# Four gated input products: one 512-column moving operand for the high weight block, the two result halves added when PSUM is emptied

## The reference, cut to what matters

```python
def swiglu_2(x, w_gate, w_up, w_down):
    return (jax.nn.silu(x @ w_gate) * (x @ w_up)) @ w_down

    x = x + 0.5 * swiglu_2(rmsnorm_2(x, ffn1_norm), ffn1_gate, ffn1_up, ffn1_down)
    ...
    x = x + 0.5 * swiglu_2(rmsnorm_2(x, ffn2_norm), ffn2_gate, ffn2_up, ffn2_down)
```

## Time and profile before

| | |
|---|---|
| Time, median of 3 runs | 2870.36 us (2867.75 to 2871.41) |
| Span of the profiled execution | 2866.6 us; the median is 3.8 us above it, for what lies around the span and for the spread of runs |
| TensorE matmuls | busy 2796.4 us (98%), 23696 |
| TensorE weight loads | busy 2684.6 us (94%), 23696 |
| VectorE, ScalarE, GpSimd | 64%, 47%, 28% |

### The profile page before, as it was taken

One profiled execution on the slowest core, in us unless ns is written; L12 is line 12 of the kernel. 1 busy time (PEld: TensorE's weight loads), 2 busy tenths in 40 slices (PEclk: granted clock), 3 DMA queues, 4 the chain that ended last, 5 costly groups with the idle time before them and its releaser, 6 DMA issues.

```text
span 2866.6 us, 59491 instructions
## 1 busy us (share of the span) xinstructions
PE 2796.4 (98%) x23696; PEld 2684.6 (94%) x23696; DVE 1820.9 (64%) x2505; ACT 1341.1 (47%) x1872; POOL 789.2 (28%) x768
## 2 busy tenths in 40 slices
PE   6999999999999999999999999999999999999999
PEld 4999999999999999999987898999889999997999
DVE  4655746687647557566466765665876566488664
ACT  3434434444435444344345444445764444377443
POOL 1322411123304214133001330320743223146330
PEclk9999999999999999999999999999999999999999
DMA  8765666575666756766631454555325555541554
GB/s 304 256 243 205 231 232 209 193 248 193 235 233 204 243 202 209 240 201 230 239 104 60 147 183 154 176 193 184 131 82 186 195 174 184 192 156 60 178 183 152
DMA packets 151712, 546.44 MB, mean 191 GB/s; under 512 B 16688, under 2 KB 20576, under 8 KB 151136
## 3 DMA queue, kind: packets, MB, share of 16 engines
q1 hardware_dynamic: 147632, 534.84, 54.9%
q10 hardware_dynamic: 3888, 8.86, 0.9%
HBM read 541.80 MB, written 1.84 MB: 190 GB/s over the span
## 4 chain that ended last, share of the span: by engine, by line
PE 91%; DVE 5%; ACT 1%; issue 1%; ACTq 1%; DMA 0%; SPq 0%; DVEq 0%
PE ps L410 28%; PE ps L412 28%; PE ps L411 28%; PE ps L437 2%; DVE w_lo L390 1%; PE ps L821 1%; PE ps L805 1%; PE ps L794 1%; ACTq L1558 0%; DVE xT L1952 0%; DVE h_lo L1602 0%; DVE xT L1968 0%; PE ps L889 0%; PE ps L696 0%; DVE m L1967 0%
## 5 line engine op out<-in xcount | busy, mean ns | idle before, releaser
L390 DVE TENSOR_TENSOR w_lo<-raw,w_hi 128x1024 fp32r<-128x1024 f32 x874 | 1135.4, 1315 | 634.5 <-ACT w_hi L382 632.1
L410 PE MATMUL ps<-h_hi,w_hi 128*128 128x256 f32 (+1 forms) x4928 | 1405.8, 285 | 24.3 <-DVE h_lo L1602 12.2
L412 PE MATMUL ps<-h_hi,w_lo 128*128 128x256 f32 (+1 forms) x4928 | 1393.8, 283 | 0.0
L411 PE MATMUL ps<-h_lo,w_hi 128*128 128x256 f32 (+1 forms) x4928 | 1388.5, 282 | 0.0
L382 ACT ACTIVATE w_hi<-raw 128x1024 fp32r<-128x1024 f32 x874 | 894.4, 1053 | 515.5 <-PE ps L412 514.5
L410 PEld LDWEIGHTS ps<-h_hi,w_hi 128*128 128x128 f32 x4928 | 929.9, 189 | 45.2 <-issue 25.2
L412 PEld LDWEIGHTS ps<-h_hi,w_lo 128*128 128x128 f32 x4928 | 947.9, 192 | 0.0
L411 PEld LDWEIGHTS ps<-h_lo,w_hi 128*128 128x128 f32 x4928 | 932.2, 189 | 0.8
L2266 POOL CAST u_hi<-ut 128x256 fp32r<-128x256 f32 (+1 forms) x258 | 234.3, 908 | 1370.4 <-DVE ut L1760 787.1
L410 PE MATMUL ps<-u_hi,w_hi 128*128 128x256 f32 (+1 forms) x2064 | 588.4, 285 | 0.2 <-DVE ut L1654 0.2
L411 PE MATMUL ps<-u_lo,w_hi 128*128 128x256 f32 (+1 forms) x2064 | 581.2, 282 | 0.0
(11 more groups left out here) (317 smaller groups left out, 1761.7 us busy)
## 6 DMA issues: line engine op xcount, KB each, us to landing
raw<-wst SPq DMA_DIRECT2D x874, 512.0 KB, 3.4
modraw<-wmod SPq DMA_DIRECT2D x132, 512.0 KB, 5.3
headraw<-wmod SPq DMA_DIRECT2D x12, 512.0 KB, 10.0
mtab<-mixtabs ACTq DMA_DIRECT2D x2, 1673.5 KB, 7.1
xT<-xin ACTq DMA_DIRECT2D x2, 1024.0 KB, 23.6
atab<-attabs ACTq DMA_DIRECT2D x1, 1024.0 KB, 6.2
out<-xT SPq DMA_DIRECT2D x1, 1024.0 KB, 4.8
skew<-sqb ACTq DMA_DIRECT2D x1, 768.0 KB, 3.3
```

Source lines behind the costliest of these rows:

```text
L390: dve.tensor_tensor(w_lo[:, s, :], raw[:, s, :], w_hi[:, s, :], ALU.subtract).then_inc(S("lo_ready"), 1)
L410: pe.matmul(psum, wh, hi, start=start, stop=False)
L411: pe.matmul(psum, wh, lo, start=False, stop=False)
L412: return pe.matmul(psum, wl, hi, start=False, stop=stop)
```

## The change

- The high and the low part of the state stand side by side in one buffer `h_parts[:, 2, DC, 2T]`; `h_hi` and `h_lo` are its halves.
- In the four gated stages without the "shift" columns (the four of the last two layers), `wide_tile` replaces `tile`: one matmul with the high weight block as stationary operand and both state parts as a moving operand of 2 x 256 columns, into a whole bank of 512 columns, and one matmul of 256 columns with the low weight block and the high state part, added to the bank's first half. The product is then the sum of the bank's two halves.
- When both units of a pair are done, ACT copies the two banks' second halves to SBUF (one instruction, 2x256 columns), DVE adds them to the first halves (one instruction), DVE multiplies both by `rstd` (one instruction), and then Silu and the gated product follow as before. `gt`, `ut` and `sq` become three parts of one buffer `gus`, so that gate and up can be reached by one instruction.
- The splits of the next weight units move: in these stages, ACT and DVE split units n+3 and n+4 when n units are done, so that the out stage's own splits begin three units later (`ahead=5`).
- The other four products of that kind of the first layers, the shifted stage and all out stages keep `tile`.

```diff
+        def wide_tile(pe, s, k, bank, both, start, stop):
+            wh, wl = w_hi[:, s, P * k:P * (k + 1)], w_lo[:, s, P * k:P * (k + 1)]
+            pe.matmul(ps[:, bank, :].rearrange("p (a t) -> p a t", a=2), wh, both, start=start, stop=False)
+            return pe.matmul(ps[:, bank, 0:T], wl, both[:, 0, :], start=False, stop=stop)
...
             def gu_pe(c, before):
                 N, b = c["N"] + 2 * c["shift"], c["unit"]
                 first_units(c, before[1])
+                if not c["shift"]:
+                    wide_unit(b + 2, 0, 2)
+                    wide_unit(b + 3, 0, 3)
+                    with pe.Fori(1, FC // 2) as i:
+                        for j in range(2):
+                            pe.wait_ge(S("sum_made"), FC * c["wide"] + 2 * i + (j - 1))
+                            wide_unit(b + 2 * j, i, 2 * j)
+                            wide_unit(b + 2 * j + 1, i, 2 * j + 1)
+                    return
...
+            def wide_gu_act(c):
+                b = c["unit"]
+                def pair(i, j, bank):
+                    act.wait_ge(S("unit_done"), b + 2 * j + 2 + 4 * i)
...
+                    act.activation(gus[:, 0:3:2, j, T:2 * T], ps[:, bank:bank + 2, T:2 * T],
+                                   ACT.Copy).then_inc(S("low_copied"), 1)
+                    split_hi(act, b + 2 * j + 5, i)
+                    act.wait_ge(S("gate_scaled"), FC * c["fin"] + 2 * i + (j + 1))
+                    act.activation(gt[:, j, 0:T], gt[:, j, 0:T], ACT.Silu).then_inc(S("silu_done"), 1)
+                    split_hi(act, b + 2 * j + 6, i)
...
+            def wide_gu_dve(c):
+                d, hid = c["unit"], c["hid"]
+                def pair(i, j, bank):
+                    both = gus[:, 0:3:2, j, 0:T]
+                    dve.wait_ge(S("low_copied"), FC * c["wide"] + 2 * i + (j + 1))
+                    dve.tensor_tensor(both, ps[:, bank:bank + 2, 0:T], gus[:, 0:3:2, j, T:2 * T],
+                                      ALU.add).then_inc(S("sum_made"), 1)
+                    dve.wait_ge(S("sum_made"), FC * c["wide"] + 2 * i + (j + 1))
+                    dve.tensor_tensor(both, both, rstd[:, 0:T].unsqueeze(1).broadcast_to([P, 2, T]),
+                                      ALU.mult).then_inc(S("gate_scaled"), 1)
+                    split_lo(dve, d + 2 * j + 5, i)
+                    dve.wait_ge(S("gate_scaled"), FC * c["fin"] + 2 * i + (j + 1))
+                    dve.wait_ge(S("silu_done"), FC * c["ffn"] + 2 * i + (j + 1))
+                    dve.wait_ge(S("ulo_ready"), hid + 2 * i + (j + 1))
+                    dve.tensor_tensor(ut[:, j, 0:T], gt[:, j, 0:T], sq[:, j, 0:T], ALU.mult).then_inc(S("gated"), 1)
+                    split_lo(dve, d + 2 * j + 6, i)
```

More of the change, by code:

```diff
@@ L140, in make_plan @@
     plan = []
-    c = dict(unit=REACHED["dense"], norm=0, pre2=0, x=0, out=0, post=0, ffn=REACHED["ffn"], fin=0,
+    c = dict(unit=REACHED["dense"], norm=0, pre2=0, x=0, out=0, post=0, ffn=REACHED["ffn"], fin=0, wide=0,
              hid=REACHED["hid"], h=0, early_n=0)
@@ L158, in gu, with out @@
         c["fin"] += 1
+        c["wide"] += not shift
         c["hid"] += FC
-    def out(N, nk):
-        add("out", N=N, nk=nk)
+    def out(N, nk, ahead=2):
+        add("out", N=N, nk=nk, ahead=ahead)
         c["unit"] += nk
@@ L186, in make_plan @@
                 gu(T)
-                out(T, FC)
+                out(T, FC, 5)
             else:
@@ L714, in first_units @@
                     for n in range(2):
[L715 removed]
+                        if c["shift"]:
+                            mm = tile(pe, (b + n) % RING, k, ps[:, 4 + n, 0:N], h_hi[:, k, 0:N], h_lo[:, k, 0:N], k == 0, k == DC - 1)
+                        else:
+                            mm = wide_tile(pe, (b + n) % RING, k, 4 + n, h_parts[:, :, k, 0:T], k == 0, k == DC - 1)
                         if k == DC - 1:
@@ L718, in first_units, with wide_unit @@
                 early_stat(norm)
+            def wide_unit(d, i, bank):
+                s = d % RING
+                pe.wait_ge(S("lo_ready"), d + 4 * i + 1)
+                for k in range(DC):
+                    mm = wide_tile(pe, s, k, bank, h_parts[:, :, k, 0:T], k == 0, k == DC - 1)
+                mm.then_inc(S("unit_done"), 1)
             def gu_pe(c, before):
@@ L1314, in first_qkv_act @@
                 hi_upto(act, d + 14)
+            def wide_gu_act(c):
+                b = c["unit"]
+                def pair(i, j, bank):
+                    act.wait_ge(S("unit_done"), b + 2 * j + 2 + 4 * i)
+                    if not isinstance(i, int):
+                        act.wait_ge(S("sum_made"), FC * c["wide"] + 2 * i + (j - 1))
+                    act.activation(gus[:, 0:3:2, j, T:2 * T], ps[:, bank:bank + 2, T:2 * T],
[4 more added lines that the diff above has]
+                    split_hi(act, b + 2 * j + 6, i)
+                pair(0, 0, 4)
+                pair(0, 1, 2)
+                with act.Fori(1, FC // 2) as i:
+                    for j in range(2):
+                        pair(i, j, 2 * j)
             def gu_act(c):
+                if not c["shift"]:
+                    wide_gu_act(c)
+                    return
                 b = c["unit"]
@@ L1336, in out_act @@
             def out_act(c):
-                b, nk = c["unit"], c["nk"]
-                full = nk // 4 if b + nk + 2 <= UNITS else (nk - 2) // 4
-                with act.Fori(0, full) as i:
+                b, first = c["unit"], c["unit"] + c["ahead"]
+                n = min(b + c["nk"] + 2, UNITS) - first
+                with act.Fori(0, n // 4) as i:
                     for j in range(4):
-                        split_hi(act, b + 2 + j, i)
-                for k in range(4 * full, nk):
-                    split_hi(act, b + 2 + k)
+                        split_hi(act, first + j, i)
+                for k in range(n // 4 * 4, n):
+                    split_hi(act, first + k)
             def post_act(c):
@@ L1618, in pre2_dve @@
                 recip(c, T)
+            def wide_gu_dve(c):
[14 more added lines that the diff above has]
+                    split_lo(dve, d + 2 * j + 6, i)
+                pair(0, 0, 4)
+                pair(0, 1, 2)
+                with dve.Fori(1, FC // 2) as i:
+                    for j in range(2):
+                        pair(i, j, 2 * j)
             def gu_dve(c):
+                if not c["shift"]:
+                    wide_gu_dve(c)
+                    return
                 d = c["unit"]
@@ L1807, in out_dve @@
             def out_dve(c):
-                b, nk = c["unit"], c["nk"]
-                full = nk // 4 if b + nk + 2 <= UNITS else (nk - 2) // 4
-                with dve.Fori(0, full) as i:
+                b, first = c["unit"], c["unit"] + c["ahead"]
+                n = min(b + c["nk"] + 2, UNITS) - first
+                with dve.Fori(0, n // 4) as i:
                     for j in range(4):
-                        split_lo(dve, b + 2 + j, i)
-                for k in range(4 * full, nk):
-                    split_lo(dve, b + 2 + k)
+                        split_lo(dve, first + j, i)
+                for k in range(n // 4 * 4, n):
+                    split_lo(dve, first + k)
             def post_dve(c, follower):
```

9 lines of the change are left out of this document (4 added, 5 removed).

## The result

The changed kernel takes 2875.64 us (median of 20 runs, 2868.89 to 2878.03), the kernel before 2870.03 (20 runs). The ratio is 1.0019, with a 95% interval of 1.0013 to 1.0025: slower by 5.6 us. The interval excludes 1, but 5.6 us is still just inside the 5.7 us (0.2%) that I had set as the least that can be told from no change. I had forecast 2858.1 us and 0.53 for faster.

The account below looks back on a forecast made before the run. TensorE was taken as the bound, its gated-stage matmuls paced by weight loads. Terms of -27.1, +11.4 and +3.4 us summed to -12.3, giving 2858.1 us; the forecast's own range was 2851 to 2866, with rivals 2847 to 2886.

Parts of the forecast that it names:

- Term 1: Gated stages: with loads hidden under the wide matmul, a block falls from 353.7 to 333.5 ns, -27.1 us in all.
- the loads set the 117.9 ns: Gated stages before: each 256-column matmul is bound by its weight load, 112 ns plus a hand-over of some 6 ns.
- The loads' 112 ns: Distance between weight-load starts at 64-column matmuls, taken as the least for 128x128 loads, above the 106.7 ns of 256 columns.
- half clock: At 1.2 GHz, 256-column fp32r matmuls start 0.21 to 0.22 us apart, read as the load's extra vanishing under longer columns.
- the extra belongs to each matmul: Gated stages: the wide matmul also keeps 11.2 ns extra; 11.3 ns saved a block, 2870 us, no change; chance 0.25.
- the moving reads set the pace: Gated stages: 512 columns take 235.8 ns, nothing saved, stage ends add 14.8 us, 2885 us; chance 0.15.
- The row with 258 columns: Profile row: 24 matmuls at 120.0 ns each, 2.1 ns more for two columns, noted as speaking against a load bound.
- Term 2: Within gated stages: DVE's 4.45 us and ACT's 3.11 us per pair fit in TensorE's 5.34 us; cost nothing.
- Term 3: Gated stage start: first pair's sum ends about 2148.0, before PE asks at 2148.7; cost nothing.
- Term 4: Gated stage ends: the longer chain to the gated product idles TensorE 2.85 us, four times, +11.4 us.
- Term 5: Behind the stage-end stalls: two of four bring 3.4 us of half clock, 1.7 us lost each, +3.4 us; bounds 0 to 6.8.
- the stall of 5.31 us: Earlier TensorE idle stretch, cited as being followed by 6.8 us at half clock when estimating the clock's loss.

Follow-up runs that it names:

- e10: Changed kernel with the wide matmul's weights cut to 32, 64, 96 and 128 columns in the four gated stages; stages took 116.6 to 118.0 us.
- e4: Changed kernel with the wide matmul reading a contiguous constant buffer of 264, 320, 384, 512 columns; 384 cost 290.3 ns a block, 512 cost 346.9.
- e2: Changed kernel with the wide matmul alone taken back, the two halves still added by ACT and DVE; 2881.85 us, ratio 1.0041.
- e1: Changed kernel with 24 out matmuls in place of 12 ahead of the wait for the gated product; 2863.18 us, ratio 0.9977 of the kernel before.
- e5: Changed kernel with VectorE's gated product moved ahead of the weight split in the wide gated stages; 2872.85 us in one execution.
- e6: Changed kernel with both 24 out matmuls ahead of the wait and the gated product ahead of the split; 2862.40 us, ratio 0.9975.
- e9: Changed kernel with the narrow matmul's weights cut to 32, 64, 96 and 128 columns in the four gated stages; stages took 116.6 to 118.0 us.

## Why the prediction was wrong, point by point

- **Term 1, wide matmuls: the step that failed.** I put -27.1 us; it is -8.95. The sum went wrong where it took the 215.6 ns of a full fp32 matmul for a fp32r one of 512 columns. It takes 230, so a block saves 6.7 ns and not 20.2. The reading behind it, that the loads set the 117.9 ns, was wrong too: e10 leaves 116 to 118 ns with a quarter of the load. The loads' 112 ns were a chance neighbour of 117.9. Nor did half clock speak for the loads, as I had read the earlier trace rows: in the kernel before, at a granted clock of 0.50, the loads between full fp32 matmuls of 64 columns start 0.21 us apart too (L1069 at 2639.72: four in 0.97 us, each 0.33 long), the distance of fp32r matmuls of 256 columns. And a column of full fp32 costs 0.84 ns in that kernel (L1041 at 2087.09 and 2089.68: 216 ns from start to start at 256 columns, 430 at 512), 1.9 times the 0.442 of fp32r in e4; that it passes twice for each load is what I read from 215.6 against 106.7 ns. The measured saving lies about midway between two rivals: 11.3 ns a block if the extra belongs to each matmul (wide 224 ns), nothing if the moving reads set the pace (wide 236 ns). A matmul of 512 columns costs some 6 ns less than two of 256. What the runs show is that most of the extra goes with the columns and not with the load or the pieces; that it is the reads which hold the columns up is not shown, for no run tells them from the writes into PSUM. The row with 258 columns had spoken against the loads, and I gave it too little weight, though its 120.0 ns are not on the line of e4 either (118.6).
- **Term 2, ACT and DVE within the stage:** right. e2 shows the stage unchanged to 0.01 us with all of the new work. e4 shows where it would end: below some 91 us a stage VectorE is the bound.
- **Term 3, the stage's start:** right. The trace has no wait of TensorE for the sum (`sum_made`).
- **Term 4, the stage's end:** the mechanism right and shown by e1 and e5. The added chain is 2.37 us, not 2.85: ACT starts 0.27 behind the first out matmul, not 0.38; the multiply starts 0.04 behind the add and not 0.21; and the rows of the weight split and of the product begin some 0.08 us before the row ahead of them ends. My aside that the chain would be 1.6 us shorter without the split in the way was wrong: e5 shows 0.4 to 0.5, since the product then waits for Silu (my own numbers, Silu to 3.06 us and the product behind it, gave 0.8).
- **Term 5, the clock:** I took two falls of four; there were three, each 3.4 us at half clock. With them the ends cost 14.0 us in this execution, against 14.8 forecast. That these are so near is luck in part: four chains 0.48 us too long make 1.9 us, and one fall too few makes 1.7 the other way. One reading was loose: of the 6.8 us at half clock behind the stall of 5.31 us TensorE worked only 5.15; the rest was idle.
- The time lies within my range, 2847 to 2886, but only because that rival's 2885 set its upper end; the direction, slower, is that of the rival, which I gave 0.15. By my own 5.7 us it counts as no difference, which I gave 0.26.

## What to carry to other kernels

A price for an operation that the trace lacks is best not taken from a neighbour that differs in type, even where its number fits a simple formula: one run with the operand's length varied would have told. When an evacuation grows by a few instructions, look at the one place where the next stage waits for the last of them: within the stages 0.7 us more per pair on VectorE and on ScalarE each were free, at their ends each tenth of a us was paid, and behind three of the four the granted clock was 0.50 for 3.4 us, an estimated 1.7 us each. Here the stall was cheap to cover (e1 and e6 are 12 to 13 us below the changed kernel by their ratios), by moving work of the next stage that doesn't need the late result ahead of the wait.

## What the runs showed of the hardware that I had not expected

- At a granted clock of 1.00 a fp32r matmul takes about 0.44 ns per column and some 5 ns (117 ns at 256, 230 at 512 columns), the wide one in one piece or in two, with 416 and 480 columns (187 and 219 ns) some ns above the line through their neighbours. It does not get shorter when the weight load beside it is cut from 128 to 32 columns (116 to 118 ns in e10, 230 to 235 in e9). At half clock nothing shows on top of the columns: wide and narrow take 0.43 and 0.21 us, 0.82 to 0.84 ns a column, in the changed kernel's first pair (the last row is the window of these and the next matmul, granted clock 0.50):

```profile
1789.69 0.63 PE L417 MATMUL ps<-h_parts,w_hi 128*128 128x512 f32 x1
1790.12 0.41 PE L418 MATMUL ps<-h_parts,w_lo 128*128 128x256 f32 x1
1790.33 0.63 PE L417 MATMUL ps<-h_parts,w_hi 128*128 128x512 f32 x1
1789.69:1790.97 1.28, 1.28 (x5) 1.09 (x5) 1.28 (x4) 1.03 (x4) 1.28 (x1) 0.50 0.00 0
```

  What holds the columns back at the full clock, and why 480 are 3 ns above the line, 384 below it and 224 no cheaper than 256, stays open.
- Behind the stalls of 2.2 to 2.4 us at the ends the granted clock fell to 0.50 for 3.4 us three times of four in the changed kernel; behind those of 1.7 to 1.9 us in e5 twice of four; behind those of 0.3 to 0.9 us in e1 and e6 never. Each of these counts is of one profiled execution.
